# Two MLP norms worked in token halves, and six waits moved, in a two-block transformer kernel

## What is computed

```python
x = x + rmsnorm(merged @ w_o, norm_mix_post)
h = rmsnorm(x, norm_mlp_pre)
x = x + rmsnorm(square(relu(h @ w_up)) @ w_down, norm_mlp_post)
...
h = rmsnorm_2(x, norm_mix)            # second block
proj = h @ w_in                       # q, k, v, gates of attention and of gated linear attention
o_b = rmsnorm_2(gla_chunked(q, k, v, log_a), gla_norm) * silu(r)
merged = gate_a * (o_a @ w_up_nsa) + gate_b * (o_b @ w_up_gla)
x = x + merged @ w_out
h = rmsnorm_2(x, norm_ffn)
x = x + (silu(h @ w_ffn_gate) * (h @ w_ffn_up)) @ w_ffn_down
```

## Time and profile before

| | |
|---|---|
| median of three runs | 1456.41 us (1456.04 to 1458.48) |
| the profiled execution | 1460.8 us, its span 1458.7 us |
| PE busy | 1423.4 us, 98% of the span |
| DVE, ACT, POOL busy | 779.6, 533.2, 171.7 us |
| share of PE in the chain that ended last | 95% |
| mean granted clock of PE | 0.988 |

### The profile page before, as it was taken

The page is one execution under the profiler, slowest core; times in us unless marked ns, Lnnn a source line. Parts: engine busy times, 40 slices in busy tenths (PEclk is TensorE's granted clock), DMA queues, the critical chain, the costliest instruction groups (busy, mean ns, idle before and its releaser), DMA issues.

```text
span 1458.7 us, 17400 instructions
## 1 busy us (share of the span) xinstructions
PE 1423.4 (98%) x7259; PEld 1157.7 (79%) x7259; DVE 779.6 (53%) x1023; ACT 533.2 (37%) x742; POOL 171.7 (12%) x145
## 2 busy tenths in 40 slices
PE   7999999899999999989999999999999999999998
PEld 6888678688888888867887776777878888888887
DVE  6999574644234343267494565564545455435433
ACT  6232334533233141245543326662343222212214
POOL 1030013100000000110141612111210000000002
PEclk9999999999999999989999999999999999999999
DMA  6323224112322323313243211102232323223221
GB/s 199 107 87 102 72 87 146 57 59 87 116 87 90 112 87 98 119 58 94 87 86 117 71 58 41 48 21 67 87 116 71 102 87 109 93 88 114 88 82 63
DMA packets 134879, 129.89 MB, mean 89 GB/s; under 512 B 14689, under 2 KB 130289, under 8 KB 134769
## 3 DMA queue, kind: packets, MB, share of 16 engines
q1 hardware_dynamic: 133664, 125.11, 27.6%
q0 software_dynamic: 992, 3.47, 0.8%
q10 hardware_dynamic: 144, 0.20, 0.0%
HBM read 126.27 MB, written 2.10 MB: 88 GB/s over the span
## 4 chain that ended last, share of the span: by engine, by line
PE 95%; DVE 1%; ACT 1%; DMA 1%; POOL 1%; SPq 0%; issue 0%; ACTq 0%; DVEq 0%
PE gemm L457 74%; PE gemm L867 3%; PE gemm L565 3%; PE misc L894 2%; PE misc L913 1%; PE gemm L604 1%; PE misc L715 1%; PE gemm L660 1%; DMA w_raw<-in_w_in 1%; PE gemm L970 1%; PE gemm L883 1%; PE misc L883 1%; PE gemm L615 1%; PE gemm L809 1%; POOL w_lo L2127 0%; PE misc L513 0%
## 5 line engine op out<-in xcount | busy, mean ns | idle before, releaser
L1519 DVE TENSOR_TENSOR w_lo<-w_raw,w_hi 128x2048 fp32r<-128x2048 f32 (+1 forms) x108 | 246.6, 2283 | 189.1 <-ACT w_hi L1033 189.1
L457 PE MATMUL gemm<-h_hi,w_hi 128*128 128x512 f32 x844 | 331.7, 393 | 0.0
L457 PE MATMUL gemm<-h_hi,w_lo 128*128 128x512 f32 x844 | 329.0, 390 | 0.0
L457 PE MATMUL gemm<-h_lo,w_hi 128*128 128x512 f32 x844 | 329.0, 390 | 0.0
L1033 ACT ACTIVATE w_hi<-w_raw 128x2048 fp32r<-128x2048 f32 (+1 forms) x113 | 213.8, 1892 | 143.9 <-PE gemm L457 139.5
L457 PEld LDWEIGHTS gemm<-h_hi,w_hi 128*128 128x128 f32 x844 | 158.8, 188 | 36.2 <-issue 2.6
L457 PEld LDWEIGHTS gemm<-h_lo,w_hi 128*128 128x128 f32 x844 | 158.9, 188 | 33.0 <-issue 0.5
L457 PEld LDWEIGHTS gemm<-h_hi,w_lo 128*128 128x128 f32 x844 | 158.7, 188 | 33.2
L457 PE MATMUL gemm<-n_hi,w_hi 128*128 128x512 f32 x352 | 137.9, 392 | 1.6 <-DVE n_lo L2025 1.6
L457 PE MATMUL gemm<-n_lo,w_hi 128*128 128x512 f32 x352 | 137.4, 390 | 0.0
L457 PE MATMUL gemm<-n_hi,w_lo 128*128 128x512 f32 x352 | 137.2, 390 | 0.0
(11 more groups left out here) (420 smaller groups left out, 1832.6 us busy)
## 6 DMA issues: line engine op xcount, KB each, us to landing
w_raw<-in_w_in SPq DMA_DIRECT2D x62, 512.0 KB, 4.6
w_raw<-in_w_down SPq DMA_DIRECT2D x32, 512.0 KB, 4.4
w_raw<-in_w_up SPq DMA_DIRECT2D x28, 512.0 KB, 4.6
w_raw<-in_w_ffn_gate SPq DMA_DIRECT2D x22, 512.0 KB, 4.6
w_raw<-in_w_ffn_up SPq DMA_DIRECT2D x22, 512.0 KB, 4.7
w_raw<-in_w_ffn_down SPq DMA_DIRECT2D x16, 512.0 KB, 4.0
w_raw<-in_w_o SPq DMA_DIRECT2D x8, 512.0 KB, 4.1
w_raw<-in_w_out SPq DMA_DIRECT2D x8, 512.0 KB, 4.1
```

What stands on the lines that cost most here:

```text
L457: mm = nc.tensor.matmul(bank[:], w(s)[:, kt, col0:col0 + P], x(n), start=first, stop=last)
L1519: V.tensor_tensor(part(lo_of(s), s), part(raw_of(s), s), f(part(hi_of(s), s)), SUB).then_inc(S("lo_done"), 1)
```

## The change

The two norms are worked in halves of 256 tokens (`SIDE[0]` left, `SIDE[1]` right). The last slab of wo and of down3 no longer gives two blocks of 512 tokens but four of 256: the two left ones into `gemm2` and `gemm3`, the two right ones into `misc2` and `misc3`. The left half's mean stands behind 6 matmuls of the third, its spread ahead of the fourth. `first_up` and `first_in` run the left half of all slices and then the right one, and the right half's mean and spread lie among the left half's matmuls. DVE scales and adds, and ACT rounds, in halves as well; ACT's square of the new x stays at 512 tokens, together with the right half. The two slabs that up0 needs early are split one block earlier. The sum is one more DVE reciprocal and root for each norm.

```diff
+        def end_by_halves(name, hi, lo, q, first, last):
...
+            for n in range(first, last):
+                w, x = ((hi_of, hi), (hi_of, lo), (lo_of, hi))[n % 3]
+                mm = nc.tensor.matmul(bank[:, 0:HALF], w(s)[:, n // 3, P * (q % 2):P * (q % 2) + P], x[:, n // 3, SIDE[q // 2]],
+                                      start=n == 0, stop=n == 23)
...
+        wo_end(0, 0, 24)
+        wo_end(1, 0, 24)
+        wo_end(2, 0, 6)
         pe.wait_ge(S("sq_added"), KT)
-        mean_rows(SQA[:], True, False)
+        half_mean(0, SQA[:], True, False)
         pe.wait_ge(S("wo_squared"), KT)
-        mean_rows(SQ[1][:], False, True).then_inc(S("mean_ready"), 1)
-        spread_rstd(M[1], 1)
+        half_mean(0, SQ[1][:], False, True).then_inc(S("left_mean"), 1)
+        wo_end(2, 6, 24)
+        pe.wait_ge(S("left_inverted"), 1)
+        half_spread(0, M[1])
+        wo_end(3, 0, 24)
...
+            for half in range(2):
+                for k in range(KT):
+                    if half:
+                        pe.wait_ge(S("hhi_ready"), 2 * KT + k + 1)
+                    else:
+                        pe.wait_ge(S("hhi_left"), k + 1)
+                    for b in range(4):
+                        for w in (hi_of, lo_of):
+                            nc.tensor.matmul(G[(m + b) % 4][:, SIDE[half]], w(s + b // 2)[:, k, P * (b % 2):P * (b % 2) + P],
+                                             HHI[:, k, SIDE[half]], start=half == 0 and k == 0 and w is hi_of, stop=False)
...
+                    if half == 0 and k == 3:
+                        pe.wait_ge(S("rows_inverted"), 1)
+                        pe.wait_ge(S("right_read"), 1)
+                        half_spread(1, M[2])
```

The norm after down3 is cut in the same way, with the right half's mean behind slice 1 and its spread behind slice 5. DVE's part there, and ACT's:

```diff
+        for k in range(KT):
+            scaled_half(0, k, "norm_mlp_post")
+            if k:
+                x_half(0, k - 1, KT)
+            if k == 1:
+                add_right(1)
+            if k == 5:
+                dve.wait_ge(S("rows_rooted"), 3)
+                V.reciprocal(RSTDR[64:128, :], ROOTR[64:128, :]).then_inc(S("rows_inverted"), 1)
...
+        down_right(0)
+        u_left(0)
+        u_left(1)
+        down_right(1)
+        u_left(2)
+        u_left(3)
```

```diff
-        last_gates(13)
+        full(26)
+        nc.scalar.activation(GT[:, 14, :], G[2][:], ACT.Tanh, scale=0.5).then_inc(evac[2], 1)
...
-        split_hi(15)
+        full(27)
+        nc.scalar.activation(GT[:, 15, :], G[3][:], ACT.Tanh, scale=0.5).then_inc(evac[3], 1)
+        nc.scalar.activation(TMP16[:, 0:1], EPSB[:], ACT.Sqrt)
...
+            if k in (4, 6):
+                half(7 + k // 2, 0, lambda: v_branch(k // 2 - 2), 4)
...
-        half(10, 1)
+        half(10, 1, lambda: level(LEVELS), 2)
...
+                    if (kv, g, h) == (0, 1, 1):
+                        pool.wait_ge(S("gla_rstd"), 1)
...
-    GATE_FIRST, GATE_LAST = 12, 16
+    GATE_AHEAD, GATE_FIRST, GATE_LAST = 5, 17, 16
...
         pe.wait_ge(S("ropes_ready"), 6)
+        gate_matmuls(0, GATE_AHEAD)
...
-        for bl in (6, 7):
-            pe.wait_ge(*evac_at(mM + bl))
...
+                if j == 0 and b in (1, 2):
+                    pe.wait_ge(*evac_at(mM + 5 + b))
...
+        for b in range(2):
+            pe.wait_ge(evac[(b0 + b) % 4], (b0 + b) // 4 + 1)
+            for k in range(KT - 1):
+                pe.wait_ge(S("ffn_in_lo"), k + 1)
+                fup_part(b, k)
+        pe.wait_ge(S("ffn_in_lo"), KT)
+        for b in range(2):
+            fup_part(b, KT - 1).then_inc(S("block_full"), 1)
```

More of the change, by code:

```diff
@@ L1741, in nothing @@
             pass
-        run("wo", nothing)
-        split_lo(PH["up0"][0] + 1)
-        split_lo(PH["up0"][0] + 2)
+        s0, _, b0, _ = PH["wo"]
+        for j in range(4):
+            if j == 3:
+                for i in range(2):
+                    s = PH["up0"][0] + 1 + i
+                    dve.wait_ge(S("early_hi"), i + 1)
+                    V.tensor_tensor(lo_of(s)[:], raw_of(s)[:], f(hi_of(s)[:]), SUB)
+            split_lo(s0 + j + 1)
         def invert_rows(n):
@@ L1917, in _ @@
             rope(n)
-        dve.wait_ge(read[0], 14)
-        step.wait(dve)
-        V.reciprocal(RS4[:], RS4[:]).then_inc(S("gla_rstd"), 1)
         split(14)
```

283 lines of the change are left out of this document (209 added, 74 removed).

## The result

The changed kernel takes 1440.24 us (median of 4 executions, 1438.93 to 1442.82) beside 1456.22 for the kernel before; the ratio is 0.9882, 95% interval 0.9870 to 0.9895. The forecast was 1439.0, with 1434.5 to 1445.5 as its range. The gain was to be 17.3 us and is 16.0 by the medians. The traced execution of after took 1442.8 us, its span 1441.0, 17.7 less than the span of before.

The account below looks back on a forecast made before the run. The prediction took PE to bound the kernel (busy 98% of the span), so only its holes counted. Its terms, 5.8 + 4.4 + 2.4 + 1.8 + 1.0 + 0.3 + 0.9 + 0.7 = 17.3 us, took 1456.4 to 1439.1; range 1434.5 to 1445.5.

Parts of the forecast that it names:

- The norm behind wo: MLP norm after wo: halves remove 9.5 us excess, less 1.5 splitting and 2.2 small matmuls; gain 5.8 us, bounds 3.5 to 6.5.
- The norm behind down3: Norm after down3: excess 10.9 us, less splitting, small matmuls and 3.0 us of new waits; gain 4.4, bounds 2.5 to 6.
- Layer norm: Convolution's layer norm: PE's waits for squares (1.2 us) and reciprocal (1.1) are covered; gain 2.4 us, bounds 1.5 to 2.6.
- Levels and values: Levels and values: ACT's copies and the last level's wait covered by other matmuls; gain 1.8 us, bounds 1.2 to 2.4.
- Root: Linear attention's root: earlier reciprocal replaces the 2.7 us wait by 2.2 for the gate copy; gain 1.0, bounds 0.3 to 2.8.
- Feed-forward: Feed-forward's first blocks: the 1.6 us wait for `n_lo` stays, the short second one goes; gain 0.3 us, bounds 0 to 1.6.
- Attention: Attention: five matmuls fill the entry wait, gain 0.9 us; the end's wait for the last gate blocks is covered, gain 0.7.
- B: Rival, 17%: clock stays up behind the short waits at root and feed-forward, 1.65 and about 1.3 us more gain; 1436.
- C: Rival, 22%: halves looser than the timeline, both norms at their lower bounds and the clock drawn down once; near 1444.
- D': Rival, 7%: in `first_in`, 96 halves with 3 us of waits run at low clock, about 7 us more; 1446.
- D: Rival, 3%: repeated short waits within the halves keep the clock low; from 162 halves the change loses, 250 give 1466.
- E: Rival, 5%: halves save nothing, the same waits reappear ahead of the right half; 7.1 us gain is left, 1449.

Follow-up runs that it names:

- Experiment 6: Changed kernel with the left half of the norm behind down3 in another order on DVE, PE, ACT and POOL: 1439.49 us, ratio 0.9875.
- experiment 4: Changed kernel with DVE's reciprocal of the linear attention behind the rotary terms again, as in the kernel before: 1442.70 us, ratio 0.9897.
- experiment 11: Changed kernel with half of a slab's `w_lo` made twice, to lengthen the hole ahead of the feed-forward's slice 6: 1443.58 us, ratio 0.9898.
- experiment 3: Changed kernel with PE's order in the feed-forward's first blocks as in the kernel before: 1440.81 us, ratio 0.9882.
- experiment 1: Changed kernel with both MLP norms as before, at 512 tokens, the six other moves kept: 1448.11 us, ratio 0.993.
- experiment 5: Changed kernel with three reorderings at the waits left in feed-forward, linear attention and attention: 1436.77 us, ratio 0.9864.
- experiment 7: Kernel of Experiment 6 with ACT's squares of the new x in halves as well: 1436.63 us, ratio 0.9863.

## Why the prediction was right, term by term

- **The norm behind wo, 5.8 forecast, 4.7 measured.** The mechanism held: no waits, the clock at 1.00 throughout. Two prices were too low. The small matmuls run in four groups, which cost 0.56 + 0.64 + 0.78 + 0.64 = 2.6 us and not 2.2. (The 1.01 us for the mean in the earlier trace rows, from which the 2.2 came, lay in a stretch of low clock; at 1.00 the same 16 take 0.57.) And the 112 matmuls that were split cost 2.2 and not 1.5: the halves run at 0.120, as read from the kernel's end, but the first one behind each small group takes 0.1 us longer, and the right half of up0 takes 11.71 us for 96, 0.122 each. For the gap between matmuls the prediction weighed a rule of the Trainium skill ("TensorE: Matmul & The Clock Gate", section Back-to-back issue gap). By its fixed 2.5 ns a half would take 0.109 us; the trace has 0.120.
- **The norm behind down3, 4.4 forecast, 1.6 measured.** The step that failed is "3.0 us of new waits": they are 4.6. Ahead of slice 1 it is 1.2 us (1.05 forecast): close. In the right half it is 0.4 + 1.7 where 1.4 stood, and ahead of slice 5 it is 1.3 us where 0.5 stood. I had the right reciprocal wait for nothing but its place in DVE's list. The trace shows it wait for ACT's root, 0.61, since the mean itself came late through the first hole, and then the next add slowed by POOL from 0.42 to 1.09. I had looked at when POOL's transfers end, and not at the conversion behind them. Experiment 6 removed the holes of the left half by order alone. The waits are 1.6 of the 2.8 us that were missed. The other 1.2 are the two prices of the norm behind wo again: the small groups cost 2.7 us (0.66 + 0.64 + 0.78 + 0.64) and not 2.2, and the 96 split matmuls about 2.0 and not 1.25.
- **Layer norm, 2.4 forecast, 3.5 measured.** The two waits went as said. The variance's 32 small matmuls took 1.01 us and not 1.95: before they ran at the pace at which ACT squared. I counted the idle time and not the time that the waiting had stretched.
- **Levels and values, 1.8 forecast, 2.7 measured.** The three waits gave their 2.5 us in full. Of the 0.7 that were taken off for cutting and switching little was spent: a cut block costs next to nothing (12 + 12 matmuls in 2.96 + 2.75 us, beside 5.67 for 24 in one) where 0.2 was put down. And the last level gained more than its wait: its 32 matmuls ran in two stretches of 1.16 us and now run in one of 1.98.
- **Root, 1.0 forecast, 2.35 measured.** The wait of 1.8 us stood where and for whom it was forecast (2.2 said). The clock was the open point: the prediction's own sum is 0.5 with a new fall and 2.1 without, and it took 1.0. There was no fall. Experiments 4 and 11 have one behind 2.7 and 2.8 us.
- **Feed-forward, 0.3 forecast, 1.7 measured.** The wait of 1.6 us stayed, as said. The 1.7 us are the fall of the clock in the first trace of before: there the mean takes 1.01 us and the 24 matmuls behind it 6.76, in after 0.57 and 5.44 at that pace. Its second trace has no such fall. The 0.3 of the change itself can't be told from nothing, as experiment 3 says too.
- **Attention, 1.6 forecast, 1.3 measured,** with the unforeseen wait of 1.0 us inside it. The rest came as said: from the transposes to the gate matmuls behind the first scores 2.51 us pass in both traces, with five more matmuls in them now, and the hole of 0.8 at the end is gone. I wrote that 159 in place of 164 matmuls are left as filling, and did not follow the number that is made from them: the step at which ACT empties a block.
- **The rivals.** B was right in its mechanism at both places: the clock stayed up behind the 1.8 us wait and behind the 1.6 us of the feed-forward (there also with the old order, experiment 3). Its 1436 did not come, as down3 gave 2.8 us less and the clock fell at 840. Its price at the root was also too high: 1.65 on top of 1.0, where the sum without a fall is 2.1. C (halves looser than the timeline) was right at down3, by 2.8 us, and wrong at wo. D' and D are out. `first_in` had holes of 1.2 and 1.3 us, 5 us apart, and the clock stayed at 1.00 all through it. The Trainium skill ("TensorE: Matmul & The Clock Gate", section A second HAM failure mode) tells of an oscillation through short idle times between groups of matmuls; these two holes did not bring it. E is out by experiment 1.

So the total was right by balance, and that is luck: -1.1 and -2.8 in the norms and -0.3 in the attention against +1.1, +0.9, +1.35 and +1.4 elsewhere. The forecast named every place of a wait but one; five terms of eight were off by 1 us or more, and four (down3, layer norm, levels, feed-forward) lay outside their own bounds. By the medians the gain is 16.0 and not 17.7, as the traced execution of before lay 4.6 us above its median and that of after 2.6 above its own.

What stays open: which stretches of small matmuls bring the clock down and when. In the traces of kernels with the new order the fall behind them is at 650 to 660, at 835 to 850, or nowhere.

## What to carry to other kernels

When a norm is cut in halves, lay out the list of the elementwise engine with the end of every matmul group it waits for: an add that stands three slices too early (1.86 us of standing still), with what hangs on it, cost 2.7 us, more than the 1.6 that the halves brought there, and its place is free to choose. When a number that counts filler matmuls changes, follow everything computed from it. And price a hole for the clock as well as for its length: here the clock was low behind every hole of 2.7 us and more, which cost about 1.4 us and more each time, and behind single holes of up to 1.8 us only once. So shortening a long hole to below that is worth more than the time it saves. Last, an engine whose list is full (DVE in experiments 5 and 7) gives such gains back a few microseconds later unless its own order is changed too.

## What the hardware showed beyond the forecast

- In the kernel before, the lower clock cost 12.4 us of 1458.7 from 100 us on, and half of what the change brought was clock. An execution's time goes with its mean granted clock for the most part: the changed kernel took 1438.9 us at 1.000 and 1442.8 at 0.996, the kernel of experiment 6 1436.4 at 1.000 and 1440.6 at 0.995. Not in full: that of experiment 3 took 1441.1 and 1444.3 at 0.998.
- The same instructions with the same hole of 1.57 us met a low clock in one trace of before and a full one in the other, and a full one in the eight traces of changed kernels with a hole of that length there.
- DVE's add of 128 x 256 took 1.09 us in place of 0.42 while POOL converted 128 x 1024 to bytes, its eight `u_lo` 6.16 in place of 5.39 with the same conversion beside them (experiment 7), and its multiplication of 128 x 512 by a table 0.64 to 1.78 us beside POOL's products in the linear attention.
- The first matmul of 256 behind a group of small ones takes 0.1 us longer at full clock (0.22 in place of 0.12 to the start of the second).
